# A recurrent head's gate products end two levels earlier; second-layer logits from rounded halves; ScalarE scales the attention weights, SyncE shifts the values, and the input is turned by products

## The chip, the cores and the metric

One core of a Trainium2 chip runs the whole program. The metric is the device time of one execution in microseconds (us), as the median of several executions; lower is better. The kernel has five engines at work: PE (TensorE, matrix products), DVE (VectorE), ACT (ScalarE), POOL (GpSimd) and SP (SyncE, which here only issues DMAs). Each works through its own list of instructions in order and waits on semaphores for the others.

## What is computed

The reference is two layers over 512 tokens of 1024 features, in 32-bit floats:

```
# first layer
h = rmsnorm(x, norm_pre);  proj = h @ w_in
xbc = silu(conv1d(xbc) + conv_b);  y = ssd_scan(...)            # 16 heads, chunks
y_ssd = gated_group_rmsnorm(y, z_ssd, ssd_norm, 2) @ w_ssd_proj
o = stick_breaking(q, k, v)                                     # 16 heads
y_sb = (o * silu(z_sb)) @ w_sb_proj
x = x + rmsnorm((g_ssd * y_ssd + g_sb * y_sb) @ w_out, norm_post)
# second layer
h = rms_norm(x, norm_mix);  proj = h @ w_in_2
o_nsa = compressed, selected and window attention, gated        # 8 heads of queries, 2 groups of keys
o_hgrn = hgrn2_mixer(hq, hf, hi, hg, ...)                       # 4 recurrent heads
x = x + concat(o_nsa, o_hgrn) @ w_out_2
x = x + (silu(gate) * up) @ w_down                              # after rms_norm
```

With 512 tokens the selected blocks and the window cover all keys before a query, so both are full causal attentions with keys and values of their own.

## The kernel before, in words

A 32-bit number is split in two halves that PE reads in one pass each: a rounded one (`hi`, by ACT) and the rest (`lo`, by DVE). A product of two such numbers is then three passes over PE (hi·hi, hi·lo, lo·hi). Where PE reads plain 32-bit numbers instead, each product is two passes, and each of these takes longer; both show in a trace as MATMUL. `a_hi`/`a_lo` and `b_hi`/`b_lo` hold activations by feature chunk (8 chunks of 128 features by 512 tokens), and `whi`/`wlo` hold a block of weights of 2048 columns, in two buffers. For each block SP loads two pieces (512 KB each, `wraw`), ACT rounds them (L1150, `round_weights`) and DVE takes the rest (L1485, `rest_of_weights`); a block is 48 passes of PE over 512 columns.

The order of all work is one list, `STEPS`, made by `plan()`; each engine walks over it and does its own part of each step. `weave` mixes streams evenly. A `("gemm", n, s)` is one eighth of block n, six passes. Everything that PE does is in this order, and PE waits wherever an operand is late.

The stages that matter here are these.

- Beginning: each of four rows of tokens is squared and summed (ACT, L1263), its root is taken (DVE L1637 and L1638, ACT L1244), the row is multiplied by its factor and by `norm_pre` (DVE L1648, 1024 wide), turned by PE (L807, eight transposes), rounded by ACT (L1267) and split by DVE (L1680). After the fourth row come the 16 passes of the small product for `dt` (`a_hi,sw`) and the first block.
- Values of the stick-breaking heads: `v` is needed as differences of neighbouring tokens. ACT issues DMAs that shift each half of `v` by one token (L1229 to L1231) and POOL subtracts (L2056). The first of 64 units (16 heads by 4 rows of queries) follows. A unit is: logits by PE (L744), two sigmoids by ACT (L1291, L1292), a scan by DVE (L1926), transposes by PE (L1085), a copy by ACT, sums by PE.
- Second layer: the queries and keys are turned (`qkturn`, L839) and copied by ACT (L1398, L1402, L1403); then come the compressed attention (`cmp`, PE L744 and L887) woven with the `hi` product, and then 32 units of the two full attentions (`nsa`, 8 heads by 4 rows; BANK 4 and 5 hold the logits) woven with the recurrent heads.
- An `nsa` unit u: logits by PE, maximum by DVE (L1746, L1750), exponential by ACT (L1362), factor by DVE (L1739, L1740), scaling of two tiles by POOL (L2043), and, while unit u+2 stands in the list, transposes by PE (L906), copies by ACT (L1349, L1351) and sums by PE.
- A recurrent head h: its products `hq` and `hf` (one block, 8 slices), gates by ACT (L1168, with a change of the table of functions, ACT_TABLE_LOAD, to the sigmoid and back) and by DVE (L1567 to L1573; the last is the first operand of level 0), and ten levels 0 to 9 and the output `hout`. A level is a product by PE and a chain of four or five instructions of DVE (L1779 to L1790, L1803 to L1815). The block of head h+1 is woven with the levels of head h, and its last slice stands behind `hout` of head h.

## Time and profile before

| | us |
|---|---|
| median of three executions | 1460.55 (1459.80 to 1462.16) |
| the profiled execution, its own time | 1462.84 |
| its span in the trace | 1461.0 |
| busy: PE | 1390.3 |
| busy: DVE | 757.8 |
| busy: ACT | 582.6 |
| busy: POOL | 121.2 |

The span is the time from the first to the last instruction of the trace; 1.84 us of the profiled execution's time lie outside it. "Busy" counts a matrix product from its start to the modelled end, so that products that follow closely overlap, and PE may show as busy though some of its passes are drawn out. An idle time is shown in square brackets behind a row of the timeline, with the instruction that ended it.

### The profile page before, as it was taken

To read this page: it belongs to the slowest core of one execution; us is meant where nothing else is said; L and a number is where in the kernel's file an instruction comes from. 1 tells how busy PE (TensorE), PEld (TensorE's weight loads), DVE (VectorE), ACT (ScalarE), POOL (GpSimd) and SP (SyncE) were. 2 spreads that over 40 slices of the span, in tenths; PEclk is the share of its full clock that TensorE was granted. 3 is DMA by queue.
4 is the path that set the end of the run, shared out by engine and by line. 5 is a ranking of instruction groups with operands and counts; after the bars stand their busy time and mean duration, and the time that the engine had idled before them with its cause. 6 is when DMAs were issued, how large, how long until landed. Compare 5 with 4: busy or idle time off the path is not lost.

```text
span 1461.0 us, 17660 instructions
## 1 busy us (share of the span) xinstructions
PE 1390.3 (95%) x6909; PEld 1133.9 (78%) x6913; DVE 757.8 (52%) x1148; ACT 582.6 (40%) x1061; POOL 121.2 (8%) x87
## 2 busy tenths in 40 slices
PE   6899999998999999998899989999979999999999
PEld 4787778876888888876787767767868888888887
DVE  4775554555666553334554757557643433443443
ACT  4534333446777532234425444542332322322221
POOL 0107430011000000000000122221000000000000
PEclk9999999999999999999999999999999999999999
DMA  4221222332111254222431100000512233223322
GB/s 156 74 85 58 76 69 84 104 115 58 59 58 45 79 179 140 92 95 73 151 103 58 44 15 29 15 16 15 173 58 87 88 101 100 92 97 100 100 88 101
DMA packets 35493, 121.78 MB, mean 83 GB/s; under 512 B 3924, under 2 KB 5204, under 8 KB 35154
## 3 DMA queue, kind: packets, MB, share of 16 engines
q1 hardware_dynamic: 33744, 117.50, 24.0%
q10 hardware_dynamic: 1666, 3.14, 0.8%
q8 instruction: 56, 0.92, 0.2%
q14 instruction: 27, 0.22, 0.0%
HBM read 113.29 MB, written 4.19 MB: 80 GB/s over the span
## 4 chain that ended last, share of the span: by engine, by line
PE 82%; DVE 10%; ACT 4%; issue 2%; ACTq 1%; DMA 1%; POOL 0%; SPq 0%; DVEq 0%
PE bank L744 79%; PE bank L1085 1%; PE bank L906 1%; PE bank L807 1%; DVE wlo L1485 1%; DVE arena L1504 1%; ACT arena L1263 1%; DMA arena<-in_x 1%; ACT whi L1150 0%; DVE arena L1779 0%; DVE arena L1655 0%; DVE arena L1810 0%; ACT a_hi L1267 0%; DVE arena L1784 0%; DVE a_lo L1680 0%
## 5 line engine op out<-in xcount | busy, mean ns | idle before, releaser
L744 PE MATMUL bank<-a_hi,whi 128*128 128x512 f32 x848 | 342.2, 404 | 1.5 <-DVE arena L1933 0.9
L744 PE MATMUL bank<-a_hi,wlo 128*128 128x512 f32 x848 | 332.7, 392 | 0.0
L744 PE MATMUL bank<-a_lo,whi 128*128 128x512 f32 x848 | 332.3, 392 | 0.0
L1485 DVE TENSOR_TENSOR wlo<-wraw,whi 128x1024 fp32r<-128x1024 f32 x194 | 248.6, 1293 | 54.5 <-ACT whi L1150 49.1
L1150 ACT ACTIVATE whi<-wraw 128x1024 fp32r<-128x1024 f32 x194 | 196.9, 1044 | 183.2 <-PE bank L744 177.1
L744 PE MATMUL bank<-arena 128*128 128x128 f32 (+7 forms) x1400 | 221.0, 304 | 9.0 <-DVE arena L1784 4.9
L744 PEld LDWEIGHTS bank<-arena 128*128 128x128 f32 (+2 forms) x1400 | 175.4, 190 | 36.6 <-issue 21.3
L744 PEld LDWEIGHTS bank<-a_hi,wlo 128*128 128x128 f32 x848 | 160.4, 189 | 34.6
L744 PEld LDWEIGHTS bank<-a_hi,whi 128*128 128x128 f32 x848 | 160.8, 190 | 33.9 <-issue 2.0
L744 PEld LDWEIGHTS bank<-a_lo,whi 128*128 128x128 f32 x848 | 160.9, 190 | 31.9 <-issue 1.0
L744 PE MATMUL bank<-whi,a_hi 128*128 128x512 f32 x320 | 127.8, 400 | 6.9 <-DVE a_lo L1680 3.9
L744 PE MATMUL bank<-whi,a_lo 128*128 128x512 f32 x320 | 125.7, 393 | 0.0
L744 PE MATMUL bank<-wlo,a_hi 128*128 128x512 f32 x320 | 125.5, 392 | 0.0
L744 PE MATMUL bank<-whi,b_hi 128*128 128x512 f32 x240 | 94.5, 394 | 0.0
L744 PE MATMUL bank<-whi,b_lo 128*128 128x512 f32 x240 | 94.1, 392 | 0.0
L744 PE MATMUL bank<-wlo,b_hi 128*128 128x512 f32 x240 | 93.9, 391 | 0.0
L1926 DVE TENSOR_TENSOR_SCAN arena<-arena 128x128 f32<-128x128 f32 (+1 forms) x64 | 56.7, 888 | 67.1 <-ACT arena L1292 66.8
L744 PEld LDWEIGHTS bank<-whi,a_hi 128*128 128x128 f32 x320 | 60.6, 190 | 19.9 <-issue 7.7
L1199 ACT ACTIVATE b_hi<-arena 128x512 fp32r<-128x512 f32 x30 | 19.0, 632 | 135.6 <-DVE arena L1590 123.7
L744 PEld LDWEIGHTS bank<-whi,a_lo 128*128 128x128 f32 x320 | 60.6, 189 | 12.9
L744 PEld LDWEIGHTS bank<-wlo,a_hi 128*128 128x128 f32 x320 | 60.7, 190 | 11.9
L1580 DVE TENSOR_TENSOR arena<-arena,bank 128x512 f32<-128x512 f32 x32 | 22.0, 688 | 92.1 <-PE bank L744 92.1
(235 smaller groups left out, 1671.5 us busy)
## 6 DMA issues: line engine op xcount, KB each, us to landing
wraw<-in_wblk SPq DMA_DIRECT2D x190, 512.0 KB, 3.7
arena<-in_x SPq DMA_DIRECT2D x4, 512.0 KB, 6.0
arena<-in_x SPq DMA_DIRECT2D x1, 2048.0 KB, 8.3
spill<-arena SPq DMA_DIRECT2D x4, 512.0 KB, 6.6
arena<-spill SPq DMA_DIRECT2D x1, 2048.0 KB, 9.4
out<-arena SPq DMA_DIRECT2D x8, 256.0 KB, 2.6
arena<-arena ACTq DMA_DIRECT2D x2, 896.0 KB
arena<-in_w1k SPq DMA_DIRECT2D x1, 1024.0 KB, 7.1
```

The source lines that it names most:

```text
L744: return nc.tensor.matmul(o, lhsT, rhs, start=start, stop=stop, **kw)
L807: last = nc.tensor.transpose(bank[BANK[g]][:, P * i:P * i + P], src[:, t, c0 + P * i:c0 + P * i + P], ident)
L906: last = nc.tensor.transpose(bank[BANK_WT][:, o:o + P], np_[v % 3][:, b_, P * kb:P * kb + P], ident)
L1085: last = nc.tensor.transpose(bank[BANK_WT][:, P * kb:P * kb + P], sb_w[:, v % 3, P * kb:P * kb + P], ident)
L1150: A(whi[n % 2][:, cols], wraw[i][:, 0:cols.stop - cols.start], ACT.Copy).then_inc(s_hi, 1)
L1199: A(b_hi[:, c, :], tt[:, p % 2, :], ACT.Copy).then_inc(s_tround, 1)
L1263: A(junk[:, t, :], src[:, t, :], ACT.Square, accum_out=nss[name][:, t:t + 1]).then_inc(s_ss, 1)
L1485: v.tensor_tensor(wlo[n % 2][:, cols], wraw[i][:, 0:cols.stop - cols.start], f32(whi[n % 2][:, cols]), ALU.subtract).then_inc(s_lo, 1)
L1504: ins = v.scalar_tensor_tensor(acc[:, j:T], x_[:, 0:T - j], V("conv_w", 4 * i + 3 - j), acc[:, j:T], ALU.mult, ALU.add)
L1580: v.tensor_tensor(x, x, ps[:, :], ALU.add).then_inc(s_end["V"], 1)
L1926: v.tensor_tensor_scan(w[:, ::-1], fail[:, ::-1], sig[:, ::-1], 0.0, ALU.mult, ALU.add)\
```

## The change

It has five parts, and one list of steps that moves with them.

1. Beginning. The multiplication of a row by its factor is now a product: DVE makes a diagonal of 128 by 128 from the identity and the factors (`diag`), and PE multiplies each chunk of raw `x` with it (`feed`), which turns and scales in one. Chunk c of all four rows lies in bank c. Then each of eight `chunk` steps rounds 128 by 512 (ACT, with `norm_pre` as its scale) and splits it (DVE). `norm_pre` comes in the table `cst`, 8 columns, and its own DMA of 512 KB is gone. PE begins with 14 products of a constant tile (`WARMING`) that nobody reads, ACT with one square root, and each pass pair of the small product waits only for its own chunk.
2. Values. SP issues the six shifting DMAs, between pieces of weights (`SHIFTS`), and DVE subtracts, in four pieces for each half.
3. Logits of the second layer. Queries and keys are stacked as rounded half and rest (`q_hilo_2`, `k_hihi_2`, `k_lo_2`, `kc_hilo`), so that each product over plain numbers becomes two passes over rounded ones; the stacks are made by ACT, DVE (`qkturn`, new on DVE) and POOL (`k_hihi_2`, other half).
4. ACT multiplies the attention weights of unit u-1 by their factors, behind the exponentials of unit u; POOL has no part in a unit any more.
5. The 12 steps of the compressed attention stand in another order, with the next row's logits ahead of this row's transposes. The block of head h+1 now ends with level 7 of head h; levels 8, 9 and `hout` of head h are woven with the block of head h+2, and DVE makes the first operand of head h+1 after it has read level 8 of head h.

The core of the diff:

```diff
-    for row in normed(["x"], gap=1):
-        steps += row[::-1] if row[-1][0] != "turn" else row
+    chunks = [tile("x_t", c) for c in range(NK)]
+    for t in range(NT):
+        steps += [("norm", "x", t), ("apply", "x", t), ("feed", t)]
+    steps += [("chunk", c, g) for c, g in enumerate(chunks)]
...
-    steps += weave([("cmp", qt, i) for qt in range(NT) for i in range(3)], token("w_in_2", HI0, "hi", 0, "A"))
-    hs = []
+    cmps = sorted([("cmp", qt, i) for qt in range(NT) for i in range(3)], key=lambda s: (2 * s[1] + (0, 1, 3)[s[2]], -s[1]))
+    steps += weave(cmps, token("w_in_2", HI0, "hi", 0, "A"))
+    hs, pending = [], []
     for h in range(HH):
         levels = [("level", h, n, tile("level", (h, n))) for n in range(LEVELS + 1)] + [("hout", h, tile("hout", h))]
-        following = head(h + 1) if h + 1 < HH else []
-        hs += weave(levels, following[:-1]) + following[-1:]
+        hs += weave(pending + levels[:8], head(h + 1) if h + 1 < HH else [])
+        pending = levels[8:]
+    hs += pending
     units = range(UNITS + NSA_LAG + 1)
     steps += weave([("nsa", u) for u in units], hs, weights=[2 + min(u, UNITS - 1) // NH for u in units])
     hg = token("w_in_2", HG0, "hg", 0, "A")
@@ -227,7 +231,7 @@
...
+WARMING = 14
...
+SHIFTS = [block_of("v") + 4, block_of("v") + 5]
...
-                if t == 2:
+                if t == 1:
                     sp.dma_start(cst[:, :], dram["cst"]).then_inc(s_ident, 16)
-                    sp.dma_start(rows["x"], dram["norm_pre"]).then_inc(s_row["x"], 16)
...
+                    if i == 0 and n in SHIFTS:
+                        half = SHIFTS.index(n)
+                        src, dst = vt[:, :, 512 * half:512 * half + 512], v_before[half]
+                        sp.wait_ge(*ended(tile_of("v", (NT - 1, half))))
+                        sp.wait_ge(s_y, NT)
+                        if half == 1:
+                            sp.wait_ge(s_split, max(SPLITS.index(x) for x in SPLITS if x[:2] == ("turn", "y")) + 1)
+                        sp.dma_start(dst[1:113, :, :], src[0:112, :, :]).then_inc(s_vs[half], 16)
+                        sp.dma_start(dst[113:P, :, :], src[112:P - 1, :, :]).then_inc(s_vs[half], 16)
+                        sp.dma_start(dst[0:1, 1:NT, :], src[P - 1:P, 0:NT - 1, :]).then_inc(s_vs[half], 16)
...
+            def feed(t):
+
+                if t == 0:
+                    pe.wait_ge(s_warm, 1)
+                    for _ in range(WARMING):
+                        mm(bank[NK - 1][:, T - P:T], warm, warm, True, True)
+                pe.wait_ge(s_norm, norm_no("x", t))
+                for c in range(NK):
+                    last = mm(bank[c][:, P * t:P * t + P], xt[:, t, P * c:P * c + P], diag[:, t, :], True, True)
+                    if t == NT - 1:
+                        last.then_inc(s_tile, 1)
...
-                        rows_ = slice(HD * g, HD * g + HD)
-                        last = mm(bank[4 + 3 * g][:, 32 * r:32 * r + NCMP], qT[rows_, r, P * qt:P * qt + P],
-                                  kcT[rows_, 0:NCMP], True, True)
+                        for i in range(2):
+                            last = mm(bank[4 + 3 * g][:, 32 * r:32 * r + 32], q_hilo_2(h)[:, P * qt:P * qt + P],
+                                      kc_hilo[:, g, i, :], i == 0, i == 1)
...
-                        mm(ps, qT[:, r, P * qt:P * qt + P], kpad[g][:, :, 0:kend], True, False)
+                        mm(ps, queries, k_hihi_2[g][:, :, 0:kend], True, False)
+                        mm(ps, queries, k_lo_2[g][:, :, 0:kend], False, False)
...
-                    if t == NT - 1:
-                        cols = slice(512 * half, 512 * half + 512)
-                        act.wait_ge(*ended(g))
-                        act.wait_ge(s_vz, half + 1)
-                        act.dma_start(v_before[half][1:113, :, :], vt[0:112, :, cols]).then_inc(s_vs[half], 16)
-                        act.dma_start(v_before[half][113:P, :, :], vt[112:P - 1, :, cols]).then_inc(s_vs[half], 16)
-                        act.dma_start(v_before[half][0:1, 1:NT, :], vt[P - 1:P, 0:NT - 1, cols]).then_inc(s_vs[half], 16)
...
+                if 1 <= u <= UNITS:
+                    o = u - 1
+                    kend = P * (o // NH + 1)
+                    act.wait_ge(s_nf, o + 1)
+                    for b in range(2):
+                        c = 2 * (o % 2) + b
+                        last = A(np_[o % 3][:, b, 0:kend], np_[o % 3][:, b, 0:kend], ACT.Copy, scale=f2[:, c:c + 1])
+                    last.then_inc(s_nw, 1)
...
+            act.wait_ge(s_unit, 1)
+            A(unit_root, unit, ACT.Sqrt)
...
-                    if i < 4:
-                        A(qT[:, i, :], bank[BANK[g]][:, :], ACT.Copy, scale=V("q_norm")).then_inc(s_end["S"], 1)
-                    else:
-                        if i == 4:
-                            act.wait_ge(s_pads, 3)
-                        A(kpad[0][0:HD, i - 4, :], bank[BANK[g]][0:HD, :], ACT.Copy, scale=V("k_norm", i - 3)[0:HD, :])
-                        A(kpad[1][HD:P, i - 4, :], bank[BANK[g]][HD:P, :], ACT.Copy, scale=V("k_norm", i - 3)[HD:P, :])\
-                            .then_inc(s_end["S"], 1)
+                    for g_ in range(NG):
+                        own = slice(HD * g_, HD * g_ + HD)
+                        dst = q_hilo_2(i + 4 * g_)[own, :] if i < 4 else k_hihi_2[g_][own, i - 4, :]
+                        scale = V("q_norm") if i < 4 else V("k_norm", i - 3)
+                        last = A(dst, bank[BANK[g]][own, :], ACT.Copy, scale=scale[own, :])
+                    last.then_inc(s_qk2, 1)
                 if s[0] == "compress":
...
-                    if i > 0:
-                        dve.wait_ge(s_tile, DONE[level_tile(i - 1, LEVELS - 1)])
-                    v.tensor_tensor(hqk[0][1], hset[i % 2][0], hk_, ALU.mult).then_inc(s_hlev, 1)
+                    if i == 0:
+                        first_operand(i)
...
-                    last = v.scalar_tensor_tensor(xt[:, t, :], xt[:, t, :], r, rows["x"], ALU.mult, ALU.mult)
+                    dve.wait_ge(s_ident, 16)
+                    last = v.tensor_scalar(diag[:, t, :], ident, r, None, ALU.mult)
...
+            def qkturn(i, g):
+
+                dve.wait_ge(s_qk2, i + 1)
+                if i == 4:
+                    dve.wait_ge(s_pads, 2)
+                for g_ in range(NG):
+                    own, other = head_rows(g_)
+                    if i < 4:
+                        hi, lo = q_hilo_2(i + 4 * g_)[own, :], q_hilo_2(i + 4 * g_)[other, :]
+                    else:
+                        hi, lo = k_hihi_2[g_][own, i - 4, :], k_lo_2[g_][own, i - 4, :]
+                    scale = V("q_norm") if i < 4 else V("k_norm", i - 3)
+                    last = v.scalar_tensor_tensor(lo, bank[BANK[g]][own, :], scale[own, :], f32(hi), ALU.mult, ALU.subtract)
+                last.then_inc(s_end["V"], 1)
 
...
+            def first_operand(h):
+
+                v.tensor_tensor(hqk[0][1], hset[h % 2][0], hset[h % 2][1], ALU.mult).then_inc(s_hlev, 1)
...
+                    if h + 1 < HH:
+                        first_operand(h + 1)
...
+            def steps_of_values(half, t):
+                cols = slice(512 * half, 512 * half + 512)
+                dve.wait_ge(s_vs[half], 48)
+                ins = v.tensor_tensor(vt[:, t, cols], vt[:, t, cols], v_before[half][:, t, :], ALU.subtract)
+                if t == NT - 1:
+                    ins.then_inc(s_dv, 1)
...
+                if NT <= u < 2 * NT:
+                    steps_of_values(1, u - NT)
...
+                if s[0] == "chunk":
+                    c, g = s[1:]
+                    dve.wait_ge(s_round, TURNS.index(s) + 1)
+                    v.scalar_tensor_tensor(a_lo[:, c, :], bank[BANK[g]][:, :], cst[:, CST.at("norm_pre")][:, c:c + 1],
+                                           f32(a_hi[:, c, :]), ALU.mult, ALU.subtract).then_inc(s_split, 1)
...
-                if s[0] == "nsa" and 1 <= s[1] <= UNITS:
-                    u = s[1] - 1
-                    w = np_[u % 3][:, :, 0:P * (u // NH + 1)]
-                    pool.wait_ge(s_nf, u + 1)
-                    g_.tensor_tensor(w, w, f2[:, 2 * (u % 2):2 * (u % 2) + 2].unsqueeze(2).to_broadcast(list(w.shape)), ALU.mult)\
-                        .then_inc(s_nw, 1)
...
-                        g_.tensor_tensor(steps_, steps_, v_before[half], ALU.subtract).then_inc(s_dv, 1)
...
+                if s[0] == "qkturn" and s[1] >= 4:
+                    b = s[1] - 4
+                    pool.wait_ge(s_qk2, s[1] + 1)
+                    pool.wait_ge(s_pads, 2)
+                    for g in range(NG):
+                        own, other = head_rows(g)
+                        if b or g:
+                            pool.wait_ge(s_k2, 2 * b + g)
+                        g_.tensor_copy(k_hihi_2[g][other, b, :], f32(k_hihi_2[g][own, b, :])).then_inc(s_k2, 1)
```

The order of instructions that `STEPS` gives, at the places that the prediction speaks of. PE at the start of the program, before (bank4, 6 and 7 take turned rows, `sw2` is the small weight):

```order
L807 MATMUL bank6<-cst,arena 128x128 x4
L744 MATMUL bank0<-a_hi,sw2 32x512
L744 MATMUL bank0<-a_lo,sw2 32x512
L744 MATMUL bank0<-a_hi,sw2 32x512
L744 MATMUL bank0<-a_lo,sw2 32x512
```

and PE at the same place now (the first row is the constant tile, the next are the first chunks of the first row of tokens):

```order
L777 MATMUL bank7<-arena 128x128 x14
L777 MATMUL bank0<-arena 128x128
L777 MATMUL bank1<-arena 128x128
L777 MATMUL bank2<-arena 128x128
L777 MATMUL bank3<-arena 128x128
L777 MATMUL bank4<-arena 128x128
L777 MATMUL bank5<-arena 128x128
L777 MATMUL bank6<-arena 128x128
```

The eight transposes of a row have become eight products of two passes each. ACT where the first half of `v` ends, before (L1224 copies `v`, L1267 rounds the turned rows of `y`):

```order
L1224 ACTIVATE arena<-bank0 128x512
L1229 DMA arena<-arena 112x4x512
L1230 DMA arena<-arena 15x4x512
L1231 DMA arena<-arena 1x3x512
L1267 ACTIVATE b_hi<-bank4 128x4x128
L1150 ACTIVATE whi1<-wraw0 128x1024
```

and now on ACT:

```order
L1274 ACTIVATE arena<-bank0 128x512
L1310 ACTIVATE b_hi<-bank6 128x4x128
L1200 ACTIVATE whi1<-wraw0 128x1024
L1310 ACTIVATE b_hi<-bank7 128x4x128
L1200 ACTIVATE whi1<-wraw1 128x1024
```

and on SP, where both shifts stand between pieces of weights:

```order
L722 DMA wraw0<-in_wblk 128x1024
L730 DMA arena<-arena 112x4x512
L731 DMA arena<-arena 15x4x512
L732 DMA arena<-arena 1x3x512
L722 DMA wraw1<-in_wblk 128x1024
L722 DMA wraw0<-in_wblk 128x1024
L730 DMA arena<-arena 112x4x512
L731 DMA arena<-arena 15x4x512
L732 DMA arena<-arena 1x3x512
L722 DMA wraw1<-in_wblk 128x1024
```

The issues have left ACT, and the second piece of a block of weights now stands behind each shift. PE ahead of level 0 of head 1, before (the row of ten is `hout` of head 0, the six rows of `whi0` are the last slice of head 1's own block, the last row is level 0 of head 1):

```order
L744 MATMUL bank2<-arena 128x128 x10
L744 MATMUL bank5<-arena 128x512
L744 MATMUL bank5<-cstb 128x2x128
L744 MATMUL bank7<-arena 128x128 x4
L906 MATMUL bank6<-cst,arena 128x128 x4
L744 MATMUL bank1<-a_hi,whi0 128x512
L744 MATMUL bank1<-a_lo,whi0 128x512
L744 MATMUL bank1<-a_hi,wlo0 128x512
L744 MATMUL bank1<-a_hi,whi0 128x512
L744 MATMUL bank1<-a_lo,whi0 128x512
L744 MATMUL bank1<-a_hi,wlo0 128x512
L744 MATMUL bank3<-arena,cst 128x512
```

and now, from that last slice of head 1's block on (the row of two at the end is level 8 of head 0):

```order
L777 MATMUL bank1<-a_hi,whi0 128x512
L777 MATMUL bank1<-a_lo,whi0 128x512
L777 MATMUL bank1<-a_hi,wlo0 128x512
L777 MATMUL bank1<-a_hi,whi0 128x512
L777 MATMUL bank1<-a_lo,whi0 128x512
L777 MATMUL bank1<-a_hi,wlo0 128x512
L777 MATMUL bank4<-rounded_arena_49,b_lo 128x512 x2
L777 MATMUL bank4<-cstb 128x2x128
L777 MATMUL bank7<-arena 128x128 x4
L950 MATMUL bank6<-cst,arena 128x128 x4
L777 MATMUL bank2<-arena 128x128 x2
L777 MATMUL bank0<-a_hi,whi1 128x512
```

Levels 8 and 9, `hout`, three slices of head 2's block and the logits of four units now stand between the last slice of head 1's block and its level 0, where before there was nothing. A row of logits also shows part 3: one plain product (two passes in the trace) before, `x2` of rounded halves now.

## Rows read from the trace of the kernel before

**Rows 1.** The profile page: busy time by engine.

```profile
PE 1390.3 (95%) x6909; PEld 1133.9 (78%) x6913; DVE 757.8 (52%) x1148; ACT 582.6 (40%) x1061; POOL 121.2 (8%) x87
```

**Rows 2.** Windows: length, busy PE PEld DVE ACT POOL, granted clock, DMA, GB/s.

```profile
0.00:27.00 27.00, 13.40 (x48) 8.71 (x49) 13.59 (x23) 14.39 (x25) 2.97 (x5) 1.00 0.49 176
...
300.00:347.00 47.00, 38.31 (x173) 30.59 (x172) 26.68 (x26) 22.94 (x42) 9.62 (x3) 0.93 0.34 102
...
818.00:1010.00 192.00, 180.13 (x1126) 141.54 (x1129) 125.68 (x313) 85.95 (x207) 40.10 (x32) 0.97 0.05 17
```

**Rows 3.** Timeline of the beginning: start us, us, what, and [idle before <-releaser].

```profile
9.97 1.06 ACT L1263 ACTIVATE arena<-arena 128x1024 f32<-128x1024 f32 x1 [1.55 <-DMA arena<-in_x]
...
18.00 1.97 PE L807 MATMUL bank<-cst,arena 128*128 128x128 f32 x8 [0.62 <-DVE arena L1648]
...
20.50 1.99 ACT L1150 ACTIVATE whi<-wraw 128x1024 fp32r<-128x1024 f32 x2
...
21.48 0.60 PE L744 MATMUL bank<-a_hi,sw 128*32 128x512 f32 x1 [1.50 <-DVE a_lo L1680]
...
21.58 2.36 DVE L1485 TENSOR_TENSOR wlo<-wraw,whi 128x1024 fp32r<-128x1024 f32 x2 [0.25 <-ACT whi L1150]
...
27.03 0.40 PE L744 MATMUL bank<-a_hi,whi 128*128 128x512 f32 x1
```

**Rows 4.** DMA throughput in 40 slices of the first 20 us.

```profile
GB/s 0 0 0 74 188 311 320 401 434 325 249 373 348 328 410 352 401 393 431 376 389 328 410 377 385 164 57 41 0 0 0 0 0 0 0 0 0 0 0 0
```

**Rows 5.** Timeline around the shift of the values.

```profile
305.56 0.60 ACT L1267 ACTIVATE b_hi<-bank 128x512 fp32r<-128x512 f32 x1 [3.88 <-issue]
...
311.90 0.66 PE L807 MATMUL bank<-cst,arena 128*128 128x128 f32 x4 [1.75 <-DVE arena L1652]
...
316.97 5.02 DVE L1485 TENSOR_TENSOR wlo<-wraw,whi 128x1024 fp32r<-128x1024 f32 x1 [1.23 <-ACT whi L1150]
...
322.50 0.68 DVE L1908 TENSOR_TENSOR rounded_arena<-arena,rounded_arena 64x512 fp32r<-64x512 f32 x1 [0.51 <-ACT rounded_arena L1276]
...
333.12 0.61 PE L744 MATMUL bank<-rounded_arena 128*128 128x384 f32 x2 [1.91 <-ACT arena L1292]
...
335.39 5.67 DVE L1926 TENSOR_TENSOR_SCAN arena<-arena 128x256 f32<-128x256 f32 x2 [0.94 <-ACT arena L1292]
...
340.26 0.69 PE L1085 MATMUL bank<-cst,arena 128*128 128x128 f32 x2 [4.05 <-DVE arena L1926]
```

**Rows 6.** Timeline of the compressed attention: its transposes and logits.

```profile
799.93 0.44 PE L887 MATMUL bank<-cst,arena 128*128 128x128 f32 x2 [0.79 <-DVE arena L1729]
803.06 1.55 PE L744 MATMUL bank<-arena 64*128 64x31 f32 x16
```

**Rows 7.** Timeline: logits of plain numbers (`arena`) and of rounded halves (`rounded_arena`).

```profile
929.60 1.02 PE L744 MATMUL bank<-arena 128*128 128x512 f32 x2
...
374.07 0.63 PE L744 MATMUL bank<-rounded_arena 128*128 128x512 f32 x2
...
878.90 0.81 PE L744 MATMUL bank<-arena 128*128 128x384 f32 x2
...
371.25 0.51 PE L744 MATMUL bank<-rounded_arena 128*128 128x384 f32 x2
```

**Rows 8.** Timeline of units and heads, 868 to 1000 us.

```profile
868.42 1.93 PE L744 MATMUL bank<-arena,cst 128*128 128x512 f32 x2 [3.40 <-DVE arena L1573]
...
997.57 1.89 POOL L2043 TENSOR_TENSOR arena<-arena,stat 128x1024 f32<-128x1024 f32 x1 [5.57 <-DVE stat L1740]
997.77 1.97 DVE L1779 TENSOR_TENSOR arena<-arena 128x256 f32<-128x256 f32 x1
```

**Rows 9.** Groups in 818 to 1010 us: xcount | busy us, mean ns of one.

```profile
L1779 DVE TENSOR_TENSOR arena<-arena 128x256 f32<-128x256 f32 x36 | 17.0, 473 | 0.1
...
L1362 ACT ACTIVATE arena<-bank,stat 128x512 f32<-128x512 f32 x16 | 10.8, 685 | 0.4 <-DVE stat L1750 0.4
...
L1351 ACT ACTIVATE arena<-bank 128x512 f32<-128x512 f32 x16 | 9.6, 599 | 37.2 <-PE bank L906 37.2
```

115 lines of the change are left out of this document (75 added, 40 removed).

## The prediction

> **What bounds the kernel now.** I read the busy times first: PE is busy for 1390 of 1461 us and DVE for 758 [rows 1]. So what counts is what PE has to do, and where PE waits. The windows by stage come next, for the three places that the change touches: the first 27 us, in which PE is busy for 13.4; the shift of the values, 300 to 347 us, with 38.3 of 47 and a granted clock of 0.93; and the two full attentions with the recurrent heads, 818 to 1010 us, with 180 of 192 [rows 2]. In this last one DVE is busy for 126 of 192 us and POOL for 40, so DVE isn't the bound on average. The timelines then say which wait ends last.
>
> In the beginning it is a chain over ACT, DVE and PE: the third row of `x` lands just before 9.97 us, the last transposes run at 18.0, the small product starts at 21.48 and the first block at 27.03 [rows 3]. The small product's first pass takes 0.60 us and the block's first 0.40, so it began at the lower of PE's two clocks (1.2 GHz) and ended at the higher (2.4 GHz); its 16 passes took 5.5 us (27.03 less 21.48).
>
> **1. Beginning.** Gone: a DMA of 512 KB, which at the 350 to 400 GB/s of this stretch [rows 4] is 1.3 to 1.5 us ahead of the last two rows of `x`; the 1024-wide multiplication; the chain of four transposed rows. New chain: the last two rows of `x` are there by about 8.5 and 9.8 us; the last square starts at about 10 (squares are 1.06 each, with sum, root and their hand-overs about 1.8 a row), the last diagonal is ready at 12.0, and the first chunk is summed at 12.3. Then eight splits by DVE at 0.68 (the pass over 512 columns in [rows 5]) are the chain: with ACT's first rounding (0.60, [rows 9]) and the rest of the small weights they end at 18.6 (12.3 + 0.6 + 8 x 0.68 + 0.3). ACT rounds the two weight pieces by 18.9 (1.99 for two), and DVE's rest of the first piece is 1.2 (2.36 for two [rows 3]): first block at 19.8 instead of 27.0. The small product hides behind the splits, two passes for each. Since the constants land a little later relative to the first block, I give back 0.2. **Term: -7.** The other end is a PE that runs these products at 1.2 GHz: a product here is two passes, a row of tokens is eight products of two passes each. The eight transposes of 1.97 us at the low clock [rows 3] make 0.24 a pass, so a row costs 3.8 us at the low clock and 1.9 at the high one; with 3.8 for each of four rows from 6.7 us on the last chunk is summed at 21.9, the block starts at 24.4 (0.6, 0.68 and 1.2 later), and the gain is some 2.5. The 14 constant products fill the time from about 1 to 5 or 7 us, as the small product filled 21.48 to 25.3 before its passes got short, so I take the fast end.
>
> The Trainium skill ("TensorE: Matmul & The Clock Gate", What's actually happening) says that an idle stretch brings the low clock back; by it the pauses between the rows of `feed` could undo the warming, and the sum would be near that of the slow end, some 4.5 us less gain. The same page (Part 4: PE-mode transpose) says that transposes don't raise the clock; the trace agrees: after the last eight the next pass still took 0.60.
>
> **2. Values.** ACT's issuing costs it 3.88 us of idle time before L1267 at 305.56; behind it stands the turning of `y`, and PE waits 1.75 at 311.90. The second issue delays the first sigmoids: PE waits 1.91 at 333.12. Then two scans take 5.67 us together while POOL subtracts, where they would take some 1.7, and PE waits 4.05 at 340.26 [rows 5]. Behind that wait the clock is low for a while: 0.07 of the window's 47 us [rows 2] is 3.3 us of lost cycles, and I take 2.9 of them as PE's delay. Together 10.6. New cost: DVE's eight subtractions of 0.68 are 5.4 us. Four lie ahead of the first sigmoid, beside PE's last slices of `v`, where DVE had rows of 5.02 us that POOL stretched from 1.2 [rows 5]; four lie between scans, in a stage where PE is the bound. On SP the three issues push the next piece of weights back: after the second shift it can be asked for only when the last tile of `v` is read, some 4 us later than before, and ACT waits about 1 us for it with the sticks behind. I give back 1.6. **Term: -9** (between -4, if SP's delay comes back on PE in full, and -11).
>
> **3. Compressed attention.** PE waits 0.79 for each of four rows' transposes, 3.1 us, and its plain products of 31 columns take 1.55 for 16, 6.2 in all [rows 6]. The new order puts another step into each wait. 64 passes over 32 columns should take some 0.06 each, 3.8; no row shows one, and the bounds are 0.03 and 0.11 (as a plain pass now), -4 to +1. I take -2. Against this `qkturn` grows: ACT has eight half passes for the queries where it had four whole ones, DVE has twelve new ones of 0.68, 8.2 us, in a stretch of some 10 us that also holds two weight passes, and the first logits wait for the last of them: +2, at most +5. **Term: -3.**
>
> **4. Logits, scaling and levels.** A plain logit product of 512 columns takes 1.02, two rounded passes 0.63; 384 columns 0.81 and 0.51 [rows 7]; by the same step 256 columns save some 0.2. Sixteen products of 512 in the last row of queries and eight in the second (24 x 0.39 = 9.4), sixteen of 384 (4.8) and eight of 256 (1.6): 15.8 us of PE. Where PE is the bound all of it comes through, where levels stand close together DVE is: 12 of 192 us are idle on PE now. I take 10.
>
> The head's change: PE waits 3.40 us at 868.42 for the first operand and then runs at the low clock (two passes in 1.93, where two plain passes of 512 take 1.02 [rows 7, 8]); that pace holds for the next products too. Another such change, to head 3, costs about 2 to 3. With 18 passes of a block, level 8, level 9, `hout` and four units between gates and level 0 the gates' table loads and three DVE instructions are hidden: -7.5, of which 2 come back as waits in the crowded last head. POOL's part of a unit is 1.89 us at full width, and it stretched L1779 from 0.42 to 1.97 [rows 8]; over the 36 of them the mean is 473 ns [rows 9], so only some 2 us in all on this line. That relief I leave to the range but for 1 us. New cost: ACT takes over 64 scalings of 0.27 to 0.60 (L1351's 599 ns for 512 columns [rows 9]), some 28 us on an engine that is busy for 86 of 192, hidden; but each now stands behind the exponentials of the next unit (2 x 0.69), and PE's transposes come two units later, so I count +2. **Term: -14.5** (-5 to -22).
>
> **Sum.** -7 - 9 - 3 - 14.5 = -33.5. Against the profiled execution's own 1462.84 (span 1461.0 and 1.84 around it) this gives 1429.3; the median of the runs lies 2.3 below that execution, so the forecast is 1427.
>
> **The rivals.**
> A. Forecast, the four terms as they are: 1427, with 1419 to 1435 around it. Chance 0.52.
> B. DVE is the bound among the levels. For it: L1784 and L1810 stand in chains, and PE waits for DVE there now. Against it: two thirds busy. Then the saved passes only lengthen waits, term 4 is -5, and the time is 1436.5. Chance 0.22.
> C. More comes: POOL's sharing with DVE costs more than the means show, since stretched instructions stand in the chain that ends last (5.02 for 1.2, 1.97 for 0.42). Term 2 is -11, term 4 is -22, and the time 1417. Chance 0.17. The Trainium skill ("SBUF — State Buffer", Who interferes with whom) has the mechanism: a DVE instruction with two inputs in SBUF and a POOL instruction that reads SBUF exclude each other for their whole length. The trace agrees: L1779 ended at 999.7, POOL's instruction at 999.5 [rows 8].
> D. Slower: the scaling on ACT. If a unit's transposes have to wait for the maximum, two exponentials and two scalings behind it, a chain of some 4.4 us at 512 columns against 5 to 6 between units now, then each of 32 units adds a wait. It decides from 33.5 / 32 = 1.05 us a unit; at 1.3 us the time is 1427 + 41 = 1468. Against it: only the last 16 units are long, and PE has six or more passes between them. Chance 0.04.
> E. The beginning stays at the low clock and `qkturn` costs its 5: gains 2.5 + 9 + 0 + 14.5 = 26, the time is 1434.5; this and small mishaps beside it reach 1443. Chance 0.05.
>
> **How the numbers follow.** The range 1413 to 1441 takes in A, nearly all of B and C and half of E. About 0.2% (3 us) is what a measurement of this kernel can tell from no change. Only D is slower: 0.04; within 0.2% lies 0.01; faster is 0.95.
>
> **What would show it.** Right: the first `a_hi,whi` product at about 20 us; no wait of PE above 1 us for a scan near 335; no POOL row beside the units; level 0 of heads 1 to 3 without idle time before it; logits as two passes in 0.63; 818 to 1010 shortened by 14 to 15 us. Wrong: first block later than 23 with passes of 0.6; DVE above 80% busy in the units' stage with more idle time on PE ahead of the levels; idle time before the transposes L950, ended by ACT L1419. A wait of ACT for a piece of weights near 333 above 3 us would break term 2.

## The result and the profile after

The changed kernel takes 1453.61 us (median of four executions, 1451.22 to 1453.84), the kernel before 1461.36 (1459.80 to 1462.55) beside it: a ratio of 0.9944, 95% interval 0.9927 to 0.9961. It is 7.75 us faster. Forecast were 1427 and a range of 1413 to 1441, so three quarters of the gain are missing.

To find where the time went, I took the start of the first product over 512 columns of the same block of weights in both traces (the blocks are the same in both, and PE is in order). Times of one profiled execution each, in us:

| stretch | before | after | difference | forecast |
|---|---|---|---|---|
| start to block 0 | 27.03 | 21.51 | -5.52 | -7 |
| block 0 to 19 (rest of layer one's first half) | 262.03 | 262.70 | +0.67 | |
| block 19 to 24 (values, first sticks) | 88.33 | 79.57 | -8.76 | -9 |
| block 24 to 51 | 389.87 | 391.49 | +1.62 | |
| block 51 to 54 (turning, compressed attention) | 52.45 | 58.00 | +5.55 | -3 |
| block 54 to 57 (units and levels) | 193.48 | 190.28 | -3.20 | -14.5 |
| block 57 to the end | 447.83 | 448.19 | +0.36 | |
| span | 1461.03 | 1451.74 | -9.29 | -33.5 |

The page and the windows of these stretches in the changed kernel (columns as in [rows 1, 2]):

```profile
PE 1383.5 (95%) x6969; PEld 1139.9 (79%) x6973; DVE 758.9 (52%) x1176; ACT 613.8 (42%) x1132; POOL 77.5 (5%) x54
```

```profile
0.00:21.51 21.51, 18.67 (x109) 14.14 (x109) 9.43 (x25) 14.01 (x26) 0.19 (x4) 1.00 0.45 159
284.21:363.78 79.57, 76.24 (x418) 63.16 (x417) 47.29 (x66) 49.35 (x101) 0.00 (x0) 1.00 0.32 95
755.27:813.26 57.99, 52.59 (x265) 42.89 (x264) 37.52 (x84) 28.46 (x47) 2.44 (x4) 0.91 0.16 55
813.26:1003.55 190.29, 168.77 (x1151) 141.56 (x1153) 119.60 (x308) 114.49 (x271) 0.00 (x0) 0.97 0.05 18
```

and of the kernel before, for the last two:

```profile
767.26:819.72 52.46, 48.34 (x266) 37.70 (x264) 27.12 (x68) 24.93 (x40) 0.00 (x0) 1.00 0.18 61
819.72:1013.20 193.48, 181.61 (x1150) 143.72 (x1152) 124.10 (x309) 85.95 (x207) 40.10 (x32) 0.97 0.05 17
```

Read the last row of each: the units' stretch has 12.8 us less of PE's busy time and is only 3.2 shorter. ACT's busy time grew from 86 to 114. In the turning stretch DVE has ten us more (27.1 to 37.5) and the granted clock fell from 1.00 to 0.91.

**Waits of PE among the units** (813 to 1003.5 us of the changed kernel; us in total, times, longest):

```profile
PE bank L777 <- DVE arena L1874: 11.0, 7, 4.2
PE bank L950 <- ACT arena L1419: 4.8, 6, 1.7
PE bank L777 <- DVEq L1840: 3.0, 2, 1.8
PE bank L777 <- DVE arena L1905: 1.6, 2, 0.8
```

L1874 is what L1784 was before: the second operand of a level. All waits together, the shorter ones not shown included, are 20.9 us, before 11.2. The longest of these waits leads to ACT, in the timeline:

```profile
936.77 1.33 ACT L1419 ACTIVATE arena<-arena,stat 128x512 f32<-128x512 f32 x2
938.00 0.60 ACT L1400 ACTIVATE arena<-bank 128x512 f32<-128x512 f32 x1
938.48 0.61 ACT L1426 ACTIVATE b_hi<-bank 128x512 fp32r<-128x512 f32 x1
...
939.12 0.69 DVE L1741 TENSOR_TENSOR b_lo<-bank,b_hi 128x512 fp32r<-128x512 f32 x1 [4.03 <-ACT b_hi L1426]
...
941.40 1.81 PE L777 MATMUL bank<-arena 128*128 128x64 f32 x8 [4.24 <-DVE arena L1874]
```

Two scalings and a copy stand ahead of the rounding of a row's turned sums. DVE waits 4.03 us for it, with the level behind, and PE 4.24 for the level. The waits view names DVE, and DVE waited for ACT. But the scalings make only a part of this wait: the sums that ACT rounds ended on PE at 937.16, and the rounding began at 938.48, so they can have cost 1.3 us of it.

**Turning of queries and keys** (timeline of the changed kernel):

```profile
768.15 0.63 PE L882 MATMUL bank<-cst,arena 128*128 128x128 f32 x4 [0.54 <-DVE b_lo L1784]
...
772.50 0.63 PE L882 MATMUL bank<-cst,arena 128*128 128x128 f32 x4 [0.50 <-DVE b_lo L1784]
...
776.37 0.47 PE L777 MATMUL bank<-whi,a_hi 128*128 128x512 f32 x1 [2.25 <-DVEq L1630]
...
779.16 1.86 PE L777 MATMUL bank<-rounded_arena,b_hi 128*128 128x32 f32 x8 [1.07 <-DVE rounded_arena L1784]
780.86 1.87 PE L777 MATMUL bank<-rounded_arena,b_lo 128*128 128x32 f32 x8
782.57 0.77 PE L777 MATMUL bank<-whi,a_hi 128*128 128x512 f32 x1
783.14 0.63 PE L777 MATMUL bank<-wlo,a_hi 128*128 128x512 f32 x1
...
803.00 0.96 PE L777 MATMUL bank<-rounded_arena,b_hi 128*128 128x32 f32 x8
803.81 1.04 PE L777 MATMUL bank<-rounded_arena,b_lo 128*128 128x32 f32 x8
804.70 0.48 PE L777 MATMUL bank<-whi,a_hi 128*128 128x512 f32 x1
```

Idle time of 4.36 us, all for DVE (L1784 makes the rests; L1630 is a gate of head 0, whose tile holds the bank that `hi` wants). Behind the last wait comes the low clock: the logits take 3.41 (779.16 to 782.57) where the same sixteen passes take 1.70 at 803.00. The twelve passes behind them take 5.27 (782.57 to 787.84) at 0.43 from start to start, where 0.23 is usual. Together 4.36 + 1.7 + 2.5 = 8.6.

### The profile page after: what moved, and what is told of

Same layout as the page of the kernel before. It is cut to its first block and busy times, and to the rows that moved or that the text cites. A ratio compares the mean times of both kernels' runs of the same rounds, so it can differ in the third digit from the quotient of the medians.

```text
span 1451.7 us, 17841 instructions
## 1 busy us (share of the span) xinstructions
PE 1383.5 (95%) x6969; PEld 1139.9 (79%) x6973; DVE 758.9 (52%) x1176; ACT 613.8 (42%) x1132; POOL 77.5 (5%) x54
## 3 DMA queue, kind: packets, MB, share of 16 engines
q10 hardware_dynamic: 576, 1.05, 0.3%
## 5 line engine op out<-in xcount | busy, mean ns | idle before, releaser
L1546 DVE TENSOR_TENSOR wlo<-wraw,whi 128x1024 fp32r<-128x1024 f32 x194 | 243.3, 1265 | 55.1 <-ACT whi L1200 49.3
L777 PE MATMUL bank<-arena 128*128 128x128 f32 (+5 forms) x1332 | 189.5, 288 | 19.4 <-DVE arena L1874 11.0
L777 PEld LDWEIGHTS bank<-arena 128*128 128x128 f32 (+1 forms) x1332 | 167.9, 193 | 29.3 <-DVE arena L1874 12.7
L2025 DVE TENSOR_TENSOR_SCAN arena<-arena 128x128 f32<-128x128 f32 (+1 forms) x64 | 52.7, 823 | 58.5 <-ACT arena L1335 58.2
L777 PEld LDWEIGHTS bank<-whi,a_lo 128*128 128x128 f32 x320 | 61.6, 193 | 13.4
```

The costliest lines, as they stand in the source:

```text
L777: return nc.tensor.matmul(o, lhsT, rhs, start=start, stop=stop, **kw)
L1546: v.tensor_tensor(wlo[n % 2][:, cols], wraw[i][:, 0:cols.stop - cols.start], f32(whi[n % 2][:, cols]), ALU.subtract).then_inc(s_lo, 1)
L2025: v.tensor_tensor_scan(w[:, ::-1], fail[:, ::-1], sig[:, ::-1], 0.0, ALU.mult, ALU.add)\
```

## The experiments

Each kernel was compared in several rounds with the kernel before on the same chip. "Old order" is that of the levels and blocks before the change. The table gives the median, the ratio to before with its 95% interval, and from the profiled execution the stretches of blocks 51 to 54 (turning) and 54 to 57 (units).

| kernel | median | ratio | turning | units |
|---|---|---|---|---|
| changed kernel | 1453.6 | 0.9944 (0.9927 to 0.9961) | 58.0 | 190.3 |
| e1_pool | 1445.1 | 0.9880 (0.9864 to 0.9897) | 58.1 | 183.9 |
| e12_actload | 1450.6 | 0.9923 (0.9904 to 0.9943) | 54.1 | 190.5 |
| e14_actlast | 1452.7 | 0.9942 (0.9927 to 0.9956) | 57.8 | 189.6 |
| e2_order | 1449.8 | 0.9922 (0.9902 to 0.9942) | 54.1 | 189.1 |
| e3_pool_order | 1449.6 | 0.9909 (0.9886 to 0.9931) | 57.9 | 186.2 |
| e8_plain | 1453.7 | 0.9943 (0.9927 to 0.9958) | 48.5 | 196.4 |
| e11_plain_pool | 1444.4 | 0.9876 (0.9861 to 0.9891) | 48.5 | 192.7 |
| e15_plain_act_old | 1451.8 | 0.9934 (0.9919 to 0.9949) | 48.5 | 197.3 |
| e9_two | 1445.0 | 0.9889 (0.9875 to 0.9904) | 48.5 | 192.5 |
| b1_actscale | 1464.2 | 1.0021 (1.0012 to 1.0031) | 52.4 | 195.0 |
| b2_order | 1463.9 | 1.0007 (0.9995 to 1.0018) | 52.4 | 196.3 |
| e4_keys | 1451.5 | 0.9932 (0.9913 to 0.9951) | 55.6 | 192.3 |
| e10_spread_pool | 1444.0 | 0.9880 (0.9863 to 0.9896) | 53.0 | 185.4 |
| e13_bank | 1439.0 | 0.9838 (0.9821 to 0.9855) | 49.7 | 185.7 |
| e6_warm0 | 1456.0 | 0.9957 (0.9942 to 0.9972) | 58.1 | 190.3 |
| e16_poolsub | 1453.6 | 0.9947 (0.9931 to 0.9964) | 57.8 | 191.3 |

**e1_pool: scaling back on POOL.**

```diff
-                    act.wait_ge(s_nf, o + 1)
-                    for b in range(2):
-                        c = 2 * (o % 2) + b
-                        last = A(np_[o % 3][:, b, 0:kend], np_[o % 3][:, b, 0:kend], ACT.Copy, scale=f2[:, c:c + 1])
-                    last.then_inc(s_nw, 1)
...
+                    pool.wait_ge(s_nf, u + 1)
+                    g_.tensor_tensor(w, w, f2[:, 2 * (u % 2):2 * (u % 2) + 2].unsqueeze(2).to_broadcast(list(w.shape)), ALU.mult)\
+                        .then_inc(s_nw, 1)
```

> The changed kernel with the scaling of the attention weights back on POOL, all else as changed. The stage of the units (190.5 us in the changed kernel, PE idle about 23 of it) is read. Theory T: ACT's queue is the new wait. It holds 64 scalings of up to 0.67 us each, the transposes wait 4.8 us for them, and ACT's rounding of the turned sums and the gates' sigmoids come late, so that the chain of levels on DVE is late too (waits of 4.2 and 2.7 us). Without them the stage is 4 to 9 us shorter: 1445 to 1450. Rival U: DVE itself or the new order of the levels is the wait; then ACT's relief is worth no more than the 4.8 us for the transposes, POOL's sharing with DVE takes it back, and the time is 1452 to 1458.

1445.1, the best the theory allowed: scaling on ACT costs 8.5 us by the medians, 6.4 of them in the units' stretch of the profiled executions. The wait for L1419 is gone and the waits for levels are shorter (the same line is L1866 here):

```profile
PE bank L777 <- DVE arena L1866: 9.3, 7, 3.0
PE bank L777 <- DVEq L1832: 1.8, 2, 1.3
```

Whether ACT is late because it is occupied, or the transposes because they depend on it, this run doesn't say. The next two do.

**e12_actload: scaling on POOL, and useless copies of the same widths on ACT.**

```diff
                     for b in range(2):
...
+                        if u > 1:
+                            act.wait_ge(s_load, 2 * (u - 2) + b + 1)
+                        A(mem(94, [T]).bitcast(BF16)[:, T * b:T * b + kend], f32(k_hihi_2[0][:, b, 0:kend]), ACT.Copy).then_inc(s_load, 1)
```

> The changed kernel with the scaling on POOL (1445.1 as measured), and ACT copies in the same place as much as it scaled before (64 copies of the same widths, of keys into a spare place that nobody reads), waiting for nobody. It tells the two ways apart in which ACT's scaling can cost. Theory T (occupation of ACT's queue: what stands behind the scalings, the turned sums and the gates, is late): the units' stage is 188 to 191 and the time 1450 to 1454. Rival S (dependence: the transposes wait for the scaled weights, which ACT delivers later than POOL; my prediction's mechanism): the stage stays at 184 to 186, the time at 1444 to 1447.

The units' stretch is 190.5, 6.6 us longer than e1_pool's: all of the 6.4 that e1_pool had won is gone, though no other engine waits for these copies. They occupy ACT for 22.5 us, the scalings for 28.5. The two windows, e1_pool first:

```profile
813.56:997.45 183.89, 170.35 (x1155) 142.95 (x1153) 122.95 (x308) 85.99 (x207) 40.10 (x32) 0.96 0.06 18
```

```profile
808.45:998.95 190.50, 171.10 (x1150) 143.73 (x1153) 122.89 (x308) 108.48 (x271) 40.11 (x32) 0.96 0.06 18
```

POOL and DVE are as busy in both; only ACT differs, 86.0 and 108.5. PE waits for levels in it (12.5 us in nine waits, 9.3 in seven in e1_pool). Occupation of ACT's queue is enough for the loss, at 57% busy.

**e14_actlast: the same scalings, behind the copy and the rounding.**

```diff
+                if 0 <= v < UNITS:
+                    read_turned(v, 1)
+                if w >= 0 and w % NH == NH - 1:
...
                 if 1 <= u <= UNITS:
                     o = u - 1
...
-                if 0 <= v < UNITS:
-                    read_turned(v, 1)
-                if w >= 0 and w % NH == NH - 1:
```

> The changed kernel with ACT's scaling at the end of its part of a unit, behind the second copy of the turned weights and behind the rounding of the turned sums (it stood ahead of both). The same work on the same engine: only what stands behind it changes. Theory T (what stands behind the scalings in ACT's queue is late): the copies and the rounding come 0.5 to 1.3 us earlier, PE's wait of 4.2 us near 941 shrinks, while the gates' sigmoids stay behind the scalings: the units' stage (190.3) is 1 to 4 us shorter, 1450 to 1453. If not the place but the sum of ACT's work counts, nothing changes: 1453 to 1455; if the transposes wait for the scaled weights more, 1455 and above.

1452.7 against 1453.6, which can't be told apart. The place does change the waits: the one of 4.24 us became 3.02, which is what it is with POOL, and idle time in the stretch fell from 20.9 to 16.7. Yet the stretch is only 0.7 shorter, because PE is busy for 172.0 us instead of 168.8, at a granted clock of 0.95 instead of 0.97. In this execution the low clock took back what the place gave, so the run doesn't say that the place counts for nothing.

**The three switches.** Logits plain or stacked, scaling by POOL or ACT, old or new order: e2_order, e3_pool_order, e8_plain, e11_plain_pool, e15_plain_act_old and e9_two complete the table below. The edits restore the lines of before, as for the logits and the order:

```diff
-                            mm(ps, queries, k_hihi_2[g][:, b, 0:kend], True, False)
-                            mm(ps, queries, k_lo_2[g][:, b, 0:kend], False, False)
+                            mm(ps, qT[:, r, P * qt:P * qt + P], kpad[g][:, b, 0:kend], True, False)
...
-        hs += weave(pending + levels[:8], head(h + 1) if h + 1 < HH else [])
-        pending = levels[8:]
+        following = head(h + 1) if h + 1 < HH else []
+        hs += weave(levels, following[:-1]) + following[-1:]
```

> The changed kernel with the levels and blocks of the recurrent heads in the order of before, and the first operand of a head behind its gates again; all else as changed. Theory V: the new order is worth the 4 to 8 us that the wait of 3.4 us and the low clock behind it cost before, and without it the time is 1457 to 1462. Rival W: the new order crowds levels 8, 9 and the output of a head with the next block and its gates, and the waits for DVE L1874 (11.0 us) come from that; without it the time is 1446 to 1451.

> The changed kernel with the scaling on POOL and the old order of levels and blocks, so that of the units' stage only the rounded logits are new. POOL scaling alone made the stage of the units 183.9 us (190.3 in the changed kernel, 193.5 before) and the total 1445.1; the old order alone made it 189.1. Theory W': the new order is worth nothing in itself (its gain in the changed kernel is hidden, and was -1.2 us when undone): 182 to 185 in the stage, 1441 to 1446 in all. Rival V': ACT's queue hid its worth; with POOL scaling the wait of 3.4 us and the low clock behind it are back and cost 4 to 7: stage 188 to 191, total 1448 to 1452.

> The changed kernel with plain 32-bit queries and keys in the second layer, as before (no stacks, no new work of DVE in qkturn), all else as changed. The stretch of the turning of queries and the compressed attention lost 5.5 us against before in the changed kernel, the stage of the units gained 3.2. Theory X: the stacks cost 6 to 10 us in the first and save 10 to 12 in the second: 1453 to 1460. Rival Y: the saved passes only lengthen waits in the units' stage, so the stacks are a loss: 1443 to 1448.

> The changed kernel with plain logits, scaling on POOL and the old order of levels and blocks: of the change only the beginning, the shift of the values and the order of the compressed attention's steps are left. If the parts add up by stage (-4.9 with the idle time at 63 us, -8.7 for the values, -4.0 for the compressed attention, the units' stage as before at 193.5) the time is 1443 to 1445, about 8 to 10 us below the changed kernel. Rival: these gains need the rest of the change (the low clock wanders to other places), and it is 1449 or more.

> The changed kernel with plain logits and the scaling on POOL; new beginning, values, order of the compressed attention, order of levels and blocks. With stacks and POOL it is 1445.1; plain with POOL and the old order of levels is 1445.0. Theory (the parts add up: with plain logits PE is busier and the new order is worth nothing or -1, as alone on the kernel before, +2.8 in the stage): 1445 to 1448. Rival (the new order is worth 4.5 with POOL scaling whatever the logits, as with the stacks): 1440 to 1442.

> The changed kernel with plain logits and the old order of levels and blocks, scaling on ACT. It completes the table of three switches: with plain logits, POOL and the old order 1445.0; POOL and the new order 1444.4; ACT and the new order 1453.7. Theory: ACT's scaling costs much only with the new order, in which gates and levels of two heads want ACT's answers at once; with the old order it costs 0 to 3 (0.2 with stacks, 3.1 on the kernel before): 1445 to 1448. Rival: it costs 8 or more whatever the order: 1452 to 1455.

| median (units' stretch) | POOL, old | POOL, new | ACT, old | ACT, new |
|---|---|---|---|---|
| plain | 1445.0 (192.5) | 1444.4 (192.7) | 1451.8 (197.3) | 1453.7 (196.4) |
| stacked | 1449.6 (186.2) | 1445.1 (183.9) | 1449.8 (189.1) | 1453.6 (190.3) |

- ACT's scaling costs 2.9 to 6.4 us in the units' stretch in all four pairs (3.7 and 4.8 plain). My expectation for e15_plain_act_old, that the old order would hide it, was wrong (1451.8 against 1445.0 with POOL); the pair with stacks and the old order, where the medians differ by 0.2, is the exception, and there the turning stretches differ by 3.8 in the profiled executions (54.1 and 57.9).
- The stacks save 6.1 to 8.8 us among the units and cost 5.6 to 9.6 in the turning stretch. By the medians they are worth nothing with the new order; with the old one they cost 4.6 with POOL and gain 2.0 with ACT.
- The new order: -2.3 (stacked, POOL), +1.2 (stacked, ACT), +0.2 and -0.9 (plain) in the stretch. By the medians it gains 4.5 with stacks and POOL, which is where rival V' of e3_pool_order had it, and that run's stretch of 186.2 fits neither of its two theories. e2_order's 1449.8 lies where theory W had it, but not for W's reason: its waits for levels fell (L1872, 5.1 us) and one of 4.8 for the gates' operand came in their place, and of the 5.9 us between the profiled executions 3.9 come from the turning stretch, at which it changes nothing.
- e9_two has only the new beginning, the values and the new order of the compressed attention, and with 1445.0 it is 8.6 us faster than the whole change. These three parts carry twice its gain.

**b1_actscale and b2_order: one part each, on the kernel before.**

> The kernel before with one part of the change: ACT scales the attention weights, POOL doesn't. Theory T (ACT's queue is the new wait): the units' stage, 193.5 us, grows by 4 to 8, the time is 1465 to 1470, with idle time of PE before the transposes ended by ACT. Rival: in the kernel before the plain logits give ACT room and POOL's stretching of DVE goes, so the stage is 0 to 3 us shorter: 1458 to 1461.

> The kernel before with one part of the change: the block of head h+1 ends with level 7 of head h, and the first operand of a head is made behind level 8. Theory V (my prediction's term): the waits at the head's changes go, 5 us less after 2 are given back, 1455 to 1457. Rival W: levels 8, 9 and hout now stand beside the next block and wait for DVE more: 1460 to 1463.

By the ratios b1_actscale is 3.1 us slower than before; its units' stretch grew by 1.5, less than in the four pairs above and less than the 4 to 8 of theory T. b2_order is 1.0 slower with an interval that includes no change; it isn't faster, where my term had it at -5.5 by itself. In b2_order's trace the wait of 3.40 us [rows 8] is gone; waits of 3.02 and 1.75 us for a level's operand stand at 947.16 and 976.20. Idle time in the units' stretch is 10.2 us against 11.2, so less than before, and still the stretch is 2.8 longer: PE is busy for 185.3 us instead of 181.6, at a granted clock of 0.96 instead of 0.97.

**e4_keys, e10_spread_pool, e13_bank: the turning stretch.** The first lets the compressed attention wait for the queries alone. The second (with scaling on POOL) moves the two turnings of keys as well, the third also starts `hi` in another bank:

```diff
-                        pe.wait_ge(*ended(tile_of("turn_qk", 5)))
+                        pe.wait_ge(*ended(tile_of("turn_qk", 3)))
...
+    cmps[7:7] = [("qkturn", 5, tile("turn_k", 5))]
+    cmps[4:4] = [("qkturn", 4, tile("turn_k", 4))]
...
+    groups = {..., "turn_k": (6,), "hi": (3, 2, 1, 0), ...}
```

> The changed kernel, but the first logits of the compressed attention wait only for the queries' stacks (qkturn 3), and the first unit of the full attentions for the keys' (qkturn 5). In the changed kernel PE waits 1.07 us there for the last key, behind a wait of 2.25 us for the bank of hi, and 32 products behind it run at the low clock (about 4 us lost). Theory: without the second wait the clock stays high: 3 to 5 us less, 1449 to 1451. Rival: the first wait alone brings the low clock, or DVE only shifts the wait to the softmax of the first row: 0 to 1 us less, 1453.

> The changed kernel with the scaling on POOL (1445.1), and the two steps that turn and stack the keys moved from the crowd of qkturn steps into the compressed attention (as its 5th and 9th step, in a bank of their own), which then waits for the queries alone. The stretch of turning and compressed attention is 58 us with the stacks and 48.5 without. Theory: DVE's queue of twelve rest products is what PE waits for there (2.25 and 1.07 us) and what brings the low clock; with four of them moved the stretch is 50 to 54 and the time 1438 to 1442. Rival: the waits only wander, the stretch is 56 or more and the time 1444 to 1446.

> The changed kernel with scaling on POOL and the keys' turning spread (1444.0), and the products of hi begin in bank 3 instead of bank 0, which the gates of head 0 still hold. In 1444.0's trace PE waits 2.85 us for that bank at 773.45. Theory: that wait goes and the low clock behind it: the stretch of turning and compressed attention is 48 to 51 us (53.0), the time 1439 to 1442. Rival: the queries' rests are the true wait, the stretch stays above 52: 1443 to 1445.

e4_keys took 2.4 us off the stretch and its profiled execution gave 2.0 back among the units; 1451.5 can't be told from 1453.6. e10_spread_pool has the stretch at 53.0 as expected, but the median of 1444.0 misses the expected 1438 to 1442 and is only 1.1 below e1_pool's. The two profiled executions differ by 5.0 (1442.2, the fastest of its four, and 1447.2, the slowest of e1_pool's), so the low clock of a single execution is a part of the 5.1 between their stretches. In e10_spread_pool PE still waits 2.85 us for the bank that head 0's gates hold. e13_bank has that gone and one wait of 0.62 left in its place:

```profile
773.77 1.03 PE L779 MATMUL bank<-rounded_arena,b_hi 128*128 128x32 f32 x8 [0.62 <-DVE b_lo L1779]
```

The stretch is 49.7 with a granted clock of 1.00, 1.2 above that with plain logits. With 1439.0 us it is the fastest kernel here: 22.5 below the kernel before, 14.6 below the changed one.

**e6_warm0: no constant products at the start** (`WARMING = 0`).

> The changed kernel without the 14 constant products at the beginning. In it the products of the first row of x ran behind them and the first block began at 21.5 us. Theory: without them PE is idle until 6.8 us and the rows of feed and the small product run partly at the low clock, but most of that hides behind the eight splits of DVE (0.67 each, to 20.3): the first block at 22 to 24, the time 1454 to 1456. Rival: they carry the gain: first block at 24 or later, 1456 to 1459. Rival 2: they do nothing: 21.5, 1453.6.

The first block begins at 22.75 instead of 21.51. The 64 passes over raw `x` then need 9.99 us from 6.78 on. The fourteen products are worth 1.2 us at that place, where I had put 7 - 2.5 = 4.5 between the two clocks.

**e16_poolsub: the subtraction of the values back on POOL.**

```diff
+                        g_.tensor_tensor(steps_, steps_, v_before[half], ALU.subtract).then_inc(s_dv, 1)
...
-                if NT <= u < 2 * NT:
-                    steps_of_values(1, u - NT)
...
-                    for t in range(NT):
-                        steps_of_values(0, t)
```

> The changed kernel with the subtraction of the shifted values back on POOL, one instruction for each half as before; SP still issues the shifts. The stretch of the values (block 19 to block 24) took 88.3 us before and 79.6 in the changed kernel. If POOL's stretching of DVE was the greater part of the loss, as I priced it (PE's wait of 4.05 us for two scans and the low clock behind it, about 7 of 10.6), the stretch is 85 to 87 us and the time 1458 to 1461. If ACT's issuing of the DMAs was the greater part, it is 81 to 83 us and 1455 to 1457.

Neither of the two expected cases came: 1453.6 and a stretch of 79.8, as with DVE. POOL still stretches DVE's instructions:

```profile
309.10 4.61 POOL L2152 TENSOR_TENSOR arena<-arena 128x2048 f32<-128x2048 f32 x1 [0.49 <-DMA arena<-arena]
309.25 5.54 DVE L1546 TENSOR_TENSOR wlo<-wraw,whi 128x1024 fp32r<-128x1024 f32 x1 [1.22 <-ACT whi L1200]
...
327.36 4.88 POOL L2152 TENSOR_TENSOR arena<-arena 128x2048 f32<-128x2048 f32 x1 [13.65 <-DMA arena<-arena]
...
330.27 3.37 DVE L2023 TENSOR_TENSOR_SCAN arena<-arena 128x512 f32<-128x512 f32 x2 [2.42 <-ACT arena L1335]
```

The Trainium skill ("SBUF — State Buffer", Who interferes with whom) says that two such instructions exclude each other for their whole length. The trace agrees (5.54 us where 1.20 is usual, and it ends 1.1 after POOL's), but here it sets nothing: PE waits 3.2 us in the whole stretch and 3.3 in the changed kernel. The longest, 2.18 at 330.66, is for a copy by ACT (L1344), and ACT had waited 2.23 for a piece of weights ahead of it. So the move of the issues off ACT is enough for the whole gain. Whether DVE's subtraction, with the issues left on ACT, would have given a part of it wasn't run. Before, ACT stood behind its own issues ahead of the first sigmoids:

```profile
327.32 0.70 ACTq L1229 DMA_DIRECT2D arena<-arena  x1
328.04 0.91 ACTq L1230 DMA_DIRECT2D arena<-arena  x1
328.98 1.95 ACTq L1231 DMA_DIRECT2D arena<-arena  x1
331.33 1.28 ACT L1291 ACT_TABLE_LOAD   x1 [4.04 <-issue]
```

With the sticks late by that, POOL's second subtraction (335.14 before) fell on scans that PE waited for.

## Why the prediction was wrong, by its own steps

**Beginning, -7: right in mechanism, 1.5 too large, and 0.7 of it lost later.** The chain is the one described, in the timeline of the changed kernel:

```profile
11.09 1.04 ACT L1306 ACTIVATE arena<-arena 128x1024 f32<-128x1024 f32 x1
...
12.87 0.29 DVE L1709 TENSOR_SCALAR arena<-cst,stat 128x128 f32<-128x128 f32 x1 [0.27 <-ACT stat L1287]
...
13.99 4.74 ACT L1471 ACTIVATE a_hi<-bank,cst 128x512 fp32r<-128x512 f32 x8 [0.95 <-PE bank L777]
...
15.58 4.69 DVE L2040 SCALAR_TENSOR_TENSOR a_lo<-bank,cst,a_hi 128x512 fp32r<-128x512 f32 x7
20.20 2.35 DVE L1546 TENSOR_TENSOR wlo<-wraw,whi 128x1024 fp32r<-128x1024 f32 x2
...
21.51 0.47 PE L777 MATMUL bank<-a_hi,whi 128*128 128x512 f32 x1 [0.54 <-issue]
```

The last square begins at 11.09 (forecast 10), the last diagonal is ready at 13.2 (12.0), the splits end at 20.3 (18.6). Then PE waits 6.07 us at 63.47 for the decays, where it waited 5.17 before: that chain didn't move as far.

**Values, -9: near in size (-6.7 to -8.8), wrong in its larger reason.** The stretch was 88.3 us in the profiled execution of before, but 86.3 and 86.5 in b1_actscale and b2_order, which run the same instructions there. Of the 8.8 us, 5.3 are idle time of PE (8.6 before, 3.3 now); the rest goes with the granted clock (0.96 and 1.00). I put 7 of 10.6 on POOL's stretching of scans; e16_poolsub shows that it costs nothing once ACT no longer issues. SP's delay, priced at 1.6, shows as forecast: ACT waits for the piece of weights behind the second shift, and PE for a copy that stands behind it in ACT's order:

```profile
329.18 1.06 ACT L1200 ACTIVATE whi<-wraw 128x1024 fp32r<-128x1024 f32 x1 [1.33 <-DMA wraw<-in_wblk]
...
331.63 0.52 PE L1133 MATMUL bank<-cst,arena 128*128 128x128 f32 x3 [1.28 <-ACT arena L1344]
```

**Compressed attention, -3: the step that failed is the price of `qkturn`, "+2, at most +5".** The new order of the steps gave 4.0 (48.5 with plain logits, 52.45 before), as forecast 3.1. The sixteen passes over 32 columns take 1.70, 0.11 each, no less than plain ones [rows 6]: near the bound of +1 instead of -2. The stacks cost 9.5 in the stretch with ACT and the new order (5.6 in e2_order, by another course of the clock). I had counted DVE's 8.2 us beside PE's 10 and looked only at the last of them. What was missing is that the gates of head 0 stand behind them in DVE's order and hold a bank, and that 4.4 us of idle time bring 4.2 more at the low clock. e13_bank shows that neither has to be.

**Logits, scaling and levels, -14.5: found -3.2.** Three sub-terms:
- Saved passes, -10: measured -6.1 with ACT, -8.8 with POOL. Nearly right.
- Head's change, -5.5: measured -2.3 at best, +2.8 on the kernel before. The wait of 3.40 us goes, as forecast, and comes back at other levels and as passes at the low clock. I had given back 2 for the crowding of levels 8, 9 and `hout` beside the next block and its gates; that this crowding is the cause is likely, but no run separates it.
- ACT's scaling, +2 and -1 for POOL's relief: measured +6.4. The failed sentence is "some 28 us on an engine that is busy for 86 of 192, hidden". e12_actload shows that occupation alone costs as much. POOL's relief is real in DVE's busy time (119.6 against 122.9 in e12_actload) and worth nothing: with POOL's 40 us in place e12_actload's stretch is 190.5, without them the changed kernel's is 190.3 (its ACT has 6 us more to do, which may hide a little of the relief).

**The rivals.** B foresaw that saved passes would turn into waits (1436.5), but for DVE at its bound; DVE's busy time fell, and what e1_pool and e12_actload show in its place is ACT's queue. D named ACT's scaling as the mechanism that could make the change slow, but as a dependence at 1.05 us a unit; occupation alone is enough for the 6.4 / 32 = 0.2 us a unit that were measured. C, more relief from POOL, is refuted twice (e12_actload, e16_poolsub). E had `qkturn` at its 5. What came is a part of B, of D and of E together, and I had no case in which they add.

Of the signs, first block near 20 us came 1.5 late, no POOL rows beside the units and logits as two passes came, level 0 of heads 1 to 3 has no idle time before it; the shortening of 818 to 1010 by 14 did not come. The sign against, "idle time before the transposes L950, ended by ACT L1419", stood in the trace with 4.8 us.

What stays open: which part of ACT's 22 to 28 us counts. e14_actlast moved it behind one copy and one rounding and shortened the waits, but not the time; the gates' sigmoids, with four loads of tables of 1.28 us for each head, would be next and weren't tried.
